# Moving the conditioning vector's products from TensorE's attention loop to GpSimd

## The chip, the cores and the metric

One core of a Trainium2 chip runs one program. Its engines are TensorE (PE in the profile; PEld is its weight load), VectorE (DVE), ScalarE (ACT), GpSimd (POOL) and SyncE (SP). They run at the same time and wait for each other by semaphores only. The metric is the device time of one execution in microseconds (us), lower is better.

## The reference, cut to what matters

Two transformer blocks, batch 1, 512 positions, width 1024, all fp32. The change concerns the modulation of the second block, which is made from the conditioning vector `c` alone:

```python
c_act = jax.nn.silu(c)                                   # 1 x 1024
mod = (c_act @ w_ada[l] + b_ada[l])[:, None, :]          # w_ada: 1024 x 6144
shift1, scale1, gate1, shift2, scale2, gate2 = jnp.split(mod, 6, axis=-1)
h = rmsnorm(x, norm1_w[l]) * (1.0 + scale1) + shift1
...
x = x + gate1 * mix
h = rmsnorm(x, norm2_w[l]) * (1.0 + scale2) + shift2
x = x + gate2 * peer(h, ...)
```

`mod` doesn't depend on the first block. It is needed for the first time when the second block begins.

## The kernel before, in words

The kernel works through stages, one after the other: projection ("win"), retention and compression ("cmp"), compressed attention, the attention loop, the output products ("wout"), the up and down products of the first feed-forward, and then the second block: its input products ("win2"), its states, output products ("wout2"), queries and expert products. Barriers end some of the stages (`PHASE_ENDS`).

Dense products run in a precision of three products: each fp32 weight chunk of 128 x 1024 is loaded by SyncE into the ring `RAW` (`load`, line 633; four slots), split by ScalarE into a high part `WH` (`split_high`, line 246) and by VectorE into a low part `WL` (`split_low`, line 254), and TensorE multiplies high by high, low by high and high by low (`mm3`, line 261). All chunks are numbered in one sequence (`PHASES`, line 45), so that the ring runs on from stage to stage; the splits run some three chunks ahead of the products (`LEAD`).

The attention loop (TensorE line 1702, ScalarE 838, VectorE 1197) goes over 64 units: 2 branches x 4 query tiles (t) x 8 heads. In step s TensorE makes the scores of unit s against t+1 key tiles (line 1706) with the mask (1709), then the transposes of unit s-1 (1737), then the product with the values of unit s-2 (1748). VectorE takes the maximum of the scores (1202), ScalarE the exponential (844), and the two take turns in copying the transposed tile out of PSUM (851, 1209). After each eighth unit VectorE scales and adds the result (1236 to 1243).

Between the scores and the transposes of a step this loop also carries the products for `mod`. `w_ada` is 48 chunks: 6 vectors v of 8 chunks k (`ada_at`, line 568: ten steps for each v, eight of them with a chunk). The silu of `c` is spread out over 128 columns and split in two parts (`CAB`, lines 825 and 1156). Each chunk takes six products of 512 columns (line 1720), so that a PSUM bank pair holds the vector, the same in all partitions. For the gates (v = 2, 5) VectorE adds it to `GATE` (line 1220), which GpSimd had filled with the bias. For the other four, ScalarE copies it to `MODROW` (859), TensorE turns it into eight columns by one-column products (1726), and VectorE adds bias and norm weight into `MOD` (1225, 1228).

Later, in the second block, `turn_act(act, "pre3", ...)` (line 899) uses MOD[:, 0:16], "pre4" (964) the rest; line 387 reads `GATE` 0 and line 1559 `GATE` 1. "pre2", "pre3", "pre4" are the transitions between two dense stages: `norm_act`, `norm_dve` (line 378) add the product to the rows of X and normalize them, `turn_pe` (line 403) transposes the four row tiles, and `turn_act`, `turn_dve` scale and split the result.

GpSimd's queue (line 688) issues a few loads, each behind a wait: among them `ROW` with "nf_post" after the first row norm (line 725), the levels (727), and later, for the expert stage, elementwise work (737, 748).

## Time and profile before

| | us |
|---|---|
| median of 3 runs | 2852.19 |
| lowest, highest | 2852.02, 2855.08 |
| the profiled execution | 2854.3 |
| its span, first to last instruction | 2852.4 |
| TensorE busy in it | 2713.1 (95%) |
| VectorE, ScalarE, GpSimd busy in it | 1506.2, 1079.0, 199.8 |

Times of the trace are in us from the start of the span. The page gives busy time by engine, the windows give it for a stretch of time together with the granted TensorE clock (1.00 is 2.4 GHz, 0.50 is 1.2 GHz). In a timeline the brackets tell how long the engine had been idle and what it had waited for. TensorE's matmul times overlap, so the distance of two starts says what one costs.

### The profile page before, as it was taken

How to read it: one execution, taken by the hardware profiler on the slowest of the kernel's cores; microseconds unless marked ns; L12 is line 12 of the kernel's file. 1: busy time of each engine (PE TensorE's matmuls, PEld its weight loads, DVE VectorE, ACT ScalarE, POOL GpSimd, SP SyncE). 2: the span in 40 equal slices, each digit the busy share in tenths (PEclk: the TensorE clock that was granted, in tenths of full speed). 3: DMA queues.
4: the chain of work that ended last, by engine and by line, in shares of the span. 5: the costliest groups of instructions: out<-in, count | busy, mean ns of one | idle time of the engine just before them, and what ended most of it. 6: DMA issues, size and time to landing. Idle time of an engine off the chain costs nothing.

```text
span 2852.4 us, 33034 instructions
## 1 busy us (share of the span) xinstructions
PE 2713.1 (95%) x12865; PEld 2252.8 (79%) x12865; DVE 1506.2 (53%) x2472; ACT 1079.0 (38%) x1464; POOL 199.8 (7%) x127
## 2 busy tenths in 40 slices
PE   7977998899998998799999999999999999999997
PEld 6866776788787886678888888888888888888886
DVE  4363554555534565467767756565424444444444
ACT  4342443433324443343333345555423333333332
POOL 0020000000000000000001233333100000000000
PEclk9986999999999999899999999999999999999999
DMA  5321342232322221233435535454656565556552
GB/s 174 96 85 52 119 133 76 80 96 96 96 89 81 89 74 45 70 119 104 130 126 152 152 124 218 160 221 162 230 204 222 184 197 202 187 187 205 196 185 81
DMA packets 142363, 392.09 MB, mean 137 GB/s; under 512 B 10944, under 2 KB 44752, under 8 KB 140688
## 3 DMA queue, kind: packets, MB, share of 16 engines
q1 hardware_dynamic: 88032, 274.86, 29.4%
q10 hardware_dynamic: 51904, 102.77, 10.4%
q0 software_dynamic: 2288, 12.54, 1.2%
q8 instruction: 96, 1.57, 0.2%
q14 instruction: 43, 0.35, 0.0%
HBM read 318.82 MB, written 71.30 MB: 137 GB/s over the span
## 4 chain that ended last, share of the span: by engine, by line
PE 92%; DVE 4%; ACT 2%; DMA 1%; issue 1%; DVEq 0%; POOL 0%; ACTq 0%; SPq 0%; POOLq 0%
PE PS L263 27%; PE PS L264 26%; PE PS L265 26%; PE PS L1868 4%; PE PS L1706 2%; PE PS L1748 1%; PE PS L1785 1%; PE PS L1737 1%; PE PS L1709 1%; PE PS L410 1%; PE PS L1846 1%; PE PS L1684 0%; DMA RAW<-in_w_in 0%; DVE X L399 0%; DMA A<-in_subk 0%
## 5 line engine op out<-in xcount | busy, mean ns | idle before, releaser
L258 DVE TENSOR_TENSOR WL<-RAW,WH 128x1024 fp32r<-128x1024 f32 x462 | 593.4, 1286 | 807.6 <-ACT WH L252 761.3
L263 PE MATMUL PS<-HH,WH 128*128 128x512 f32 x1696 | 669.2, 395 | 16.9 <-DMA A<-in_subk 6.7
L252 ACT ACTIVATE WH<-RAW 128x1024 fp32r<-128x1024 f32 x462 | 486.3, 1053 | 469.1 <-PE PS L265 448.2
L264 PE MATMUL PS<-HL,WH 128*128 128x512 f32 x1696 | 661.9, 390 | 0.0
L265 PE MATMUL PS<-HH,WL 128*128 128x512 f32 x1696 | 661.6, 390 | 0.0
L263 PE MATMUL PS<-WH,WGH 128*128 128x512 f32 x1024 | 398.5, 389 | 0.7 <-ACT ROW L987 0.7
L264 PE MATMUL PS<-WL,WGH 128*128 128x512 f32 x1024 | 398.3, 389 | 0.0
L265 PE MATMUL PS<-WH,WGL 128*128 128x512 f32 x1024 | 398.3, 389 | 0.0
L263 PEld LDWEIGHTS PS<-HH,WH 128*128 128x128 f32 x1696 | 319.8, 189 | 84.4 <-DMA A<-in_subk 7.0
L265 PEld LDWEIGHTS PS<-HH,WL 128*128 128x128 f32 x1696 | 319.4, 188 | 66.6
L264 PEld LDWEIGHTS PS<-HL,WH 128*128 128x128 f32 x1696 | 319.8, 189 | 63.6
L263 PEld LDWEIGHTS PS<-WH,WGH 128*128 128x128 f32 x1024 | 192.2, 188 | 40.9 <-ACT ROW L987 1.1
L265 PEld LDWEIGHTS PS<-WH,WGL 128*128 128x128 f32 x1024 | 192.2, 188 | 40.0
L264 PEld LDWEIGHTS PS<-WL,WGH 128*128 128x128 f32 x1024 | 192.2, 188 | 39.9
L1021 ACT ACTIVATE WGH<-A 128x512 fp32r<-128x512 f32 x128 | 80.9, 632 | 238.0 <-DVE A L1538 238.0
L263 PE MATMUL PS<-WH,HH 128*128 128x512 f32 (+1 forms) x352 | 137.1, 390 | 22.0 <-DVEq L205 20.3
L1542 DVE TENSOR_TENSOR WGL<-A,WGH 128x512 fp32r<-128x512 f32 x128 | 88.6, 692 | 94.0 <-ACT WGH L1021 94.0
L264 PE MATMUL PS<-WL,HH 128*128 128x512 f32 (+1 forms) x352 | 135.9, 386 | 0.0
L265 PE MATMUL PS<-WH,HL 128*128 128x512 f32 (+1 forms) x352 | 135.5, 385 | 0.0
L1009 ACT ACTIVATE A<-PS 128x512 f32<-128x512 f32 x128 | 125.9, 1107 | 14.4 <-PE PS L1868 14.4
L987 ACT ACTIVATE ROW<-PS 128x512 f32<-128x512 f32 x64 | 38.3, 598 | 231.7 <-PE PS L265 231.7
L1868 PEld LDWEIGHTS PS<-A 128*128 128x128 f32 x1024 | 121.7, 192 | 3.7
(316 smaller groups left out, 2942.4 us busy)
## 6 DMA issues: line engine op xcount, KB each, us to landing
RAW<-in_peer_u SPq DMA_DIRECT2D x128, 512.0 KB, 3.6
RAW<-in_peer_v SPq DMA_DIRECT2D x128, 512.0 KB, 4.1
gate_matrices<-A ACTq DMA_DIRECT2D x8, 4096.0 KB, 12.5
A<-gate_matrices ACTq DMA_DIRECT2D x32, 1024.0 KB, 7.8
A<-acts ACTq DMA_DIRECT2D x32, 1024.0 KB, 11.4
RAW<-in_w_ada SPq DMA_DIRECT2D x48, 512.0 KB, 4.1
RAW<-in_ffn_up SPq DMA_DIRECT2D x44, 512.0 KB, 3.4
acts<-GATE SPq DMA_DIRECT2D x64, 256.0 KB, 2.9
```

Of the source, the lines that this page charges most:

```text
L252: nc.scalar.activation(WHr[:, slot(c), 0:w], RAW[:, slot(c), 0:w], ACT.Copy).then_inc(sem("high_done"), 1)
L258: nc.vector.tensor_tensor(WLr[:, slot(c), 0:w], RAW[:, slot(c), 0:w], WH[:, slot(c), 0:w], ALU.subtract).then_inc(sem("low_done"), 1)
L263: nc.tensor.matmul(out, L[0], R[0], start=first, stop=False)
L264: nc.tensor.matmul(out, L[0], R[1], start=False, stop=False)
L265: return nc.tensor.matmul(out, L[1], R[0], start=False, stop=last)
L410: last = nc.tensor.transpose(PS[:, k, t * P:(t + 1) * P], src[:, t, k * P:(k + 1) * P], ident)
L987: nc.scalar.activation(ACTED[k % 4], PS[:, 5 + k % 3, :], ACT.Gelu).then_inc(sem("gelu_done"), 1)
L1009: nc.scalar.activation(dst, PS[:, b % 4, :].rearrange("p (t n) -> p t n", t=4), ACT.Copy) .then_inc(sem("gm_stored"), 1)
L1021: nc.scalar.activation(WGHr[:, v % 4, :], WF[:, v % 2, :], ACT.Copy).then_inc(sem("w_high"), 1)
L1542: nc.vector.tensor_tensor(WGLr[:, v % 4, :], WF[:, v % 2, :], WGH[:, v % 4, :], ALU.subtract)\
L1706: nc.tensor.matmul(PS[:, s % 2, 0:(t + 1) * P], QT[0:64, h, t * P:(t + 1) * P], KT[0:64, 2 * b + h // 4, 0:(t + 1) * P], start=True, stop= ...
L1868: last = nc.tensor.matmul(PS[:, b % 4, j * P:(j + 1) * P], OHA[:, r, :], OHB[:, r, :], start=True, stop=True)
```

## The change

The 48 chunks of `w_ada` leave the sequence of chunks, and with them the loads on SyncE's queue, the 48 splits on ScalarE and on VectorE, 288 products on TensorE, CAB, MODROW and the four turns of the attention loop. Instead ScalarE scales the silu of `c` by 128 (`CA`), and GpSimd does this after the attention loop: it fetches `w_ada` in 96 pieces of 128 x 512 into two buffers (`HALVES`), multiplies each by the value of `c` that belongs to its partition, and adds it to a row tile (`ADA` for four vectors, `GATE` for two). At the end each row tile must still be summed over its 128 partitions. TensorE does that with the constant matrix "mean" (all 1/128): for the four vectors ahead of the transposes of "pre3", as 32 one-column products, after which VectorE makes `MOD` in four operations; for the gates as four products of 512 columns after the second chunk of "win2", which ScalarE copies back to `GATE`. The memory of `ADA` and `HALVES` is free during wout, up and down.

```diff
-PHASES = [("win", 24), ("cmp", 8), ("ada", 6 * NK), ("wout", 8), ("up", 2 * NF), ("down", NF),
+PHASES = [("win", 24), ("cmp", 8), ("wout", 8), ("up", 2 * NF), ("down", NF),
...
+        def modulation(dve, link):
+
+            dve.wait_ge(sem("mod_summed"), 1)
+            nc.vector.tensor_tensor(MOD[:, 0:16], PS[:, 0, 0:16], par("bada", 0, 16), ALU.add)
+            link(nc.vector.tensor_tensor(MOD[:, 16:32], PS[:, 0, 16:32], par("bada", 24, 40), ALU.add))
+            nc.vector.scalar_tensor_tensor(MOD[:, 8:16], MOD[:, 8:16], 1.0, par("n1"), ALU.add, ALU.mult)
+            nc.vector.scalar_tensor_tensor(MOD[:, 24:32], MOD[:, 24:32], 1.0, par("n2"), ALU.add, ALU.mult)\
+                .then_inc(sem("mod_taken"), 1)
+
         def norm_dve(dve, link, tag):
...
+                if t == NT and tag == "pre3":
+                    modulation(dve, link)
                 if t >= 1:
                     inverse = inverse_of_rows(dve, link, tag, t - 1)
...
         def turn_pe(pe, tag, src):
+            if tag == "pre3":
+                pe.wait_ge(sem("ada_added"), 6 * 2 * NK)
+                pe.wait_ge(sem("rows_weighted"), NT * ADDED.index(tag) + 1)
+                for n in range(4 * NK):
+                    at = slice((n % NK) * P, (n % NK + 1) * P)
+                    last = nc.tensor.matmul(PS[:, 0, n:n + 1], ADA[n // NK][:, at], con("mean")[:, 0:1], start=True, stop=True)
+                last.then_inc(sem("mod_summed"), 1)
+                pe.wait_ge(sem("mod_taken"), 1)
...
-            c0 = FIRST["ada"]
-            ada = dr["w_ada"].rearrange("(k p) (v n) -> v k p n", p=P, v=6)
-            with sp.Fori(0, 6) as i:
-                for k in range(NK):
-                    load((c0 + k, i, NK), ada[i, k])
...
-            pool.wait_ge(sem("rows_weighted"), NT)
-            pool.dma_start(ROW[:, :], dr["nf_post"].partition_broadcast(P)).then_inc(sem("row_landed"), 16)
+            ada = dr["w_ada"].rearrange("(k p) (v h n) -> k v h p n", p=P, v=6, h=2)
+            pieces = [(k, v, h) for k in range(NK) for v in range(6) for h in range(2)]
+
+            def fetch(n):
+                pool.dma_start(HALVES[:, n % 2, :], ada[pieces[n]]).then_inc(sem(f"ada_landed{n % 2}"), 16)
+
+            after(pool, "attention")
+            pool.wait_ge(sem("ca_ready"), 1)
+            pool.wait_ge(sem("gb_landed"), 32)
+            fetch(0)
+            fetch(1)
+            scaled = 0
+            for n in range(len(pieces)):
+                k, v, h = pieces[n]
+                if n == 48:
+                    pool.wait_ge(sem("rows_weighted"), NT)
+                    pool.dma_start(ROW[:, :], dr["nf_post"].partition_broadcast(P)).then_inc(sem("row_landed"), 16)
+                pool.wait_ge(sem(f"ada_landed{n % 2}"), 16 * (n // 2 + 1))
+                row = GATE[:, v // 3, :] if v % 3 == 2 else ADA[MODDED.index(v)]
+                row = row[:, 512 * h:512 * h + 512]
+                if k == 0 and v % 3 < 2:
+                    ins = nc.gpsimd.tensor_scalar(row, HALVES[:, n % 2, :], CA[:, k:k + 1], None, ALU.mult)
+                else:
+                    nc.gpsimd.tensor_scalar(HALVES[:, n % 2, :], HALVES[:, n % 2, :], CA[:, k:k + 1], None, ALU.mult)\
+                        .then_inc(sem("ada_scaled"), 1)
+                    scaled += 1
+                    pool.wait_ge(sem("ada_scaled"), scaled)
+                    wait(pool, "ada_added", n - 11)
+                    ins = nc.gpsimd.tensor_tensor(row, row, HALVES[:, n % 2, :], ALU.add)
+                ins.then_inc(sem("ada_added"), 1)
+                if n + 2 < len(pieces):
+                    pool.wait_ge(sem("ada_added"), n + 1)
+                    fetch(n + 2)
...
             link(nc.scalar.activation(CA, par("c"), ACT.Silu))
-            nc.scalar.activation(CABr[:, 0], CA.unsqueeze(2).to_broadcast([P, NK, P]), ACT.Copy)\
-                .then_inc(sem("ca_high"), 1)
+            nc.scalar.activation(CA, CA, ACT.Copy, scale=float(P)).then_inc(sem("ca_ready"), 1)
...
-                v, k = ada_at(s)
-                if v < 6 and k < NK:
-                    split_high(act, (FIRST["ada"] + NK * v + k + LEAD, 0, 0))
-                elif v in (0, 1, 3, 4) and k == NK:
...
+            act.wait_ge(sem("mod_taken"), 1)
             turn_act(act, "pre3", lambda k: MOD[:, 8 + k:9 + k], lambda k: MOD[:, k:k + 1])
...
+                if m == 2:
+                    act.wait_ge(sem("gate_summed"), 1)
+                    for g in range(2):
+                        nc.scalar.activation(GATE[:, g, :].rearrange("p (a b) -> p a b", a=2), PS[:, 4 + 2 * g:6 + 2 * g, :],
+                                             ACT.Copy).then_inc(sem("gate_kept"), 1)
...
-            split_low(dve, (FIRST["wout"] + LEAD - 1, 0, 0))
             barrier(dve, "attention")
...
-                    for half in range(2):
-                        hs = slice(half * 512, (half + 1) * 512)
-                        last = mm3(PS[:, 6 + half, :], (CABr[:, 0, k, :], CABr[:, 1, k, :]),
-                                   (WHr[:, slot(c), hs], WLr[:, slot(c), hs]), k == 0, k == NK - 1)
-                    last.then_inc(sem("chunk_used"), 1)
...
+                if m == 1:
+                    for g in range(2):
+                        for h in range(2):
+                            last = nc.tensor.matmul(PS[:, 4 + 2 * g + h, :], con("mean"), GATE[:, g, 512 * h:512 * h + 512],
+                                                    start=True, stop=True)
+                    last.then_inc(sem("gate_summed"), 1)
+                if m == 10:
+                    pe.wait_ge(sem("gate_kept"), 2)
```

## Rows read from the trace of the kernel before

**Rows 1.** The page, section 1: busy us, share of the span, instructions.

```profile
PE 2713.1 (95%) x12865; PEld 2252.8 (79%) x12865; DVE 1506.2 (53%) x2472; ACT 1079.0 (38%) x1464; POOL 199.8 (7%) x127
```

**Rows 2.** Windows: us, busy time by engine (instructions), granted clock, DMA share, GB/s.

```profile
248.20:465.90 217.70, 211.04 (x1024) 157.60 (x1024) 116.91 (x184) 101.70 (x212) 0.00 (x0) 0.90 0.36 114
248.20:264.50 16.30, 16.29 (x43) 11.84 (x43) 4.85 (x8) 5.00 (x13) 0.00 (x0) 0.50 0.20 63
408.00:418.00 10.00, 9.64 (x33) 7.76 (x34) 3.07 (x8) 3.09 (x7) 0.00 (x0) 0.52 0.02 9
418.00:464.00 46.00, 44.43 (x247) 32.29 (x245) 26.00 (x38) 19.73 (x40) 0.00 (x0) 0.99 0.30 92
514.00:538.00 24.00, 14.21 (x69) 12.23 (x68) 20.14 (x33) 18.30 (x35) 0.56 (x1) 0.79 0.20 66
538.00:789.00 251.00, 245.76 (x1067) 202.88 (x1068) 134.85 (x159) 86.61 (x115) 0.00 (x0) 0.98 0.29 93
908.00:912.00 4.00, 0.23 (x1) 0.23 (x2) 3.96 (x8) 2.60 (x6) 0.00 (x0) 0.78 0.00 0
```

**Rows 3.** Timeline of VectorE in the attention loop: start us, us, line, operation.

```profile
343.89 0.69 DVE L1202 TENSOR_REDUCE MISC<-PS 128x1 f32<-128x512 f32 x1 [0.33 <-PE PS L1709]
...
347.92 0.69 DVE L1202 TENSOR_REDUCE MISC<-PS 128x1 f32<-128x512 f32 x1 [2.20 <-PE PS L1709]
...
350.53 0.69 DVE L1202 TENSOR_REDUCE MISC<-PS 128x1 f32<-128x512 f32 x1 [0.19 <-PE PS L1709]
...
376.49 0.29 DVE L1202 TENSOR_REDUCE MISC<-PS 128x1 f32<-128x128 f32 x1 [0.47 <-PE PS L1709]
...
377.47 0.29 DVE L1202 TENSOR_REDUCE MISC<-PS 128x1 f32<-128x128 f32 x1 [0.49 <-PE PS L1709]
...
391.47 0.42 DVE L1202 TENSOR_REDUCE MISC<-PS 128x1 f32<-128x256 f32 x1
...
403.18 0.42 DVE L1202 TENSOR_REDUCE MISC<-PS 128x1 f32<-128x256 f32 x1
...
423.97 0.56 DVE L1202 TENSOR_REDUCE MISC<-PS 128x1 f32<-128x384 f32 x1 [1.79 <-PE PS L1709]
...
427.44 0.56 DVE L1202 TENSOR_REDUCE MISC<-PS 128x1 f32<-128x384 f32 x1
...
458.63 0.69 DVE L1202 TENSOR_REDUCE MISC<-PS 128x1 f32<-128x512 f32 x1 [1.32 <-PE PS L1709]
```

**Rows 4.** Timeline of VectorE at the end of the attention loop.

```profile
462.77 0.20 DVE L1236 RECIPROCAL MISC<-MISC 128x8 f32<-128x8 f32 x1 [1.20 <-PE PS L1748]
...
464.66 1.22 DVE L258 TENSOR_TENSOR WL<-RAW,WH 128x1024 fp32r<-128x1024 f32 x1
```

**Rows 5.** Chain of waits (start us, us, what), and TensorE's timeline at pre3.

```profile
378.25 1.95 PE PS L1726 x16
408.36 3.53 PE PS L1726 x16
...
911.77 0.47 PE L410 MATMUL PS<-CON,A 128*128 128x128 f32 x1 [4.36 <-DVE A L393]
```

**Rows 6.** Timeline of TensorE's weight loads, line 1828, 512-column fp32 products.

```profile
1143.21 0.19 PEld L1828 LDWEIGHTS PS<-A,CON 128*128 128x128 f32 x1 [0.24 <-issue]
```

**Rows 7.** GpSimd's lines (busy us, mean ns, idle before), and DMA issues (KB, us to landing).

```profile
L748 POOL TENSOR_TENSOR X<-CON,A 128x1024 f32<-128x1024 f32 x32 | 68.6, 2143 | 131.5 <-DVE A L1529 117.0 <-ACT X L1032 14.5
...
L707 POOL COPY HH_scratch<-A 128x256 f32<-128x256 f32 x8 | 2.8, 404 | 19.4 <-PE PS L1634 19.4
...
L725 POOL DMA_DIRECT2D ROW<-in_nf_post x1 | 0.6, 561 | 339.5 <-DVE A L393 339.5
...
ROW<-in_nf_post POOLq DMA_DIRECT2D x1, 512.0 KB, 3.9
```

**Rows 8.** VectorE's lines in 790 to 899 us, then in 1650 to 2048 us.

```profile
L258 DVE TENSOR_TENSOR WL<-RAW,WH 128x1024 fp32r<-128x1024 f32 x20 | 24.5, 1226 | 76.1 <-ACT WH L252 76.1
...
L258 DVE TENSOR_TENSOR WL<-RAW,WH 128x1024 fp32r<-128x1024 f32 x54 | 85.7, 1591 | 99.5 <-ACT WH L252 89.7 <-ACT X L1032 9.9
```

46 lines of the change are left out of this document (3 added, 43 removed).

## The prediction, made before the changed kernel ran

> **What bounds the kernel now.** I read the page first: TensorE is busy for 95% of the span, GpSimd for 7% [rows 1]. Every microsecond of products is therefore a microsecond of time, unless something makes TensorE wait. Then I read the windows of the stretch that the change touches, the attention loop, from 248.2 to 465.9 us [rows 2]: 217.7 us in which TensorE is busy for 211.0 us, VectorE for 117 and ScalarE for 102, at a mean granted clock of 0.90. The loop is bound by TensorE too, and part of it runs at the lower clock level. Third, the timeline of VectorE's maximum, which follows the scores of each unit, gives the length of a step with a w_ada chunk in it and without one [rows 3]. GpSimd is an idle engine that can take work at no cost as long as nobody waits for it.
>
> **Part 1, the attention loop without the chunk products.** A step is as long as the distance of two maxima [rows 3]. Three key tiles (here called t=3, 512 keys): 343.89 to 347.92 is 4.03 us with a chunk, 347.92 to 350.53 is 2.61 us without, so a chunk's six products cost 1.42 us. t=2 with a chunk: 3.47 us, less 1.42 is 2.05. t=1: four steps with a chunk from 391.47 to 403.18 are 2.93 each, less 1.42 is 1.51. t=0 without a chunk: 376.49 to 377.47, 0.98 us. Eight units of each t and two branches: 16 x (2.61 + 2.05 + 1.51 + 0.98) = 114.4 us.
>
> Is TensorE still the last to be ready when the products are gone? From one unit's scores to its transposes lie the maximum and the exponential, and a unit's transposes come after the next unit's scores. for t=3 the bare step is 2.61 us as soon as the chunks are gone, and TensorE is busy for 44.4 of 46 us in the stretch that ends with them [rows 2]; for t=0 the 0.98 us already is the bare step. So I take the bare steps as they stand, and add what the chunks now cover:
> - The block that VectorE runs after every eighth unit (lines 1236 to 1243, some 1.9 us, the distance from 462.77 to 464.66 in [rows 4]) delays the next maximum. Behind a long step this is covered, behind t=0 and t=1 steps it is not: I take four stalls of about 1 us, 4 us (0 to 8).
> - The clock. From 248.2 to 264.5 the granted clock is 0.50, the 1.2 GHz level, although TensorE is busy for 16.29 of 16.30 us there [rows 2]; the stage before it leaves TensorE half idle. I keep these 16.3 us at the lower level. A t=0 step at that level would cost some 1.8 us instead of 0.98 (its products twice as long), so nine steps lose 0.8 us each: 8 us (3 to 30, because thinner steps may raise the clock later).
> - Both ends. The last maximum is at 458.63 [rows 3]; a step of 2.61 us after it, at 461.2, the 64 steps are used up. VectorE ends its block at 464.66 and then spends 1.22 us on a split that the change drops there [rows 4]: 3.4 us and no split. For the start, where nothing overlaps yet, I add one and a half t=0 steps, 1.4 us: 4.8 us.
>
> Sum: 114.4 + 4 + 8 + 4.8 = 131.2 us against 217.7. Part 1 is -86.5 us, with ends at -95 and -60. This also contains the four MODROW turns, their waits, and the stretches at the lower clock level that came after them (the last is 408 to 418 at 0.52 [rows 2], with the turn of line 1726 at 408.36 [rows 5]); the diff takes out the thin one-column products ahead of them. ScalarE's and VectorE's 48 splits and SyncE's 48 loads go as well: none is late in the loop, so nothing is added for them. The two operations that built CAB sit before the loop, beside the compressed scores (line 1684) that TensorE makes without them, and give nothing.
>
> **Part 2, GpSimd's 96 pieces.** They start when the attention loop ends and TensorE asks for all 96 when it has finished the down products, at 907.4 us in the times of before (the transposes start at 911.77 after 4.36 us idle [rows 5]). The stretch between the two does not change its length, so 907.4 - 465.9 = 441 us, some 4.6 us for each piece. The price of one: the multiply, one input of 512 columns, lies between the copy of 256 columns twice (0.40 x 2 = 0.8 us) and less; I take 0.7. The add, two inputs, is half of a 128x1024 one of 2.14 us mean [rows 7]: 1.07. Issuing the next fetch is 0.56 us [rows 7]. Three waits on its own semaphores, for which no row of GpSimd stands, between nothing and 0.2 us each: 0.3. That is 2.6 us; collisions with VectorE (part 4) add perhaps 0.5: 3.1. A fetch lands 3.9 us after its issue (512 KB [rows 7]; these are 256 KB), and two are in flight: two pieces take the larger of twice 3.1 and of 3.9 + 2.6 = 6.5 us, so 3.25 each and 312 us in all. GpSimd ends about 125 us before it is asked. Cost on the path: zero, cover 125 us. If that cover is gone (over 4.6 us for each piece), each further 0.1 us costs 9.6 us. The moved ROW load (nf_post) waits behind piece 48, about 160 us after the loop, while its reader comes after 435 us: nothing. The level load stands behind all pieces, as late as before. By the Trainium skill, GPSIMD Engine Reference, section Performance versus the Vector engine, elementwise work belongs on VectorE and a two-input fp32 add of 2048 columns takes 4.5 us on GpSimd; 2.14 us for 1024 columns here agrees with it. By that page the add of a piece would be an estimated 1.1 us, and the sum the same: the rule against this placement matters only where somebody waits for GpSimd.
>
> **Part 3, what TensorE gets back.** Before the transposes of "pre3" it now makes 32 one-column fp32 products, 64 passes. The 16 passes of line 1726 took 1.95 us once and 3.53 us in the stretch with a clock of 0.52 [rows 2, 5], so 64 take 7.8 or 14.1 us. TensorE has only the idle 4.36 us before 911.77 to hide them. In before the clock falls in that gap (0.78 in the mean of 908 to 912 [rows 2]), at about 910; I take 19 passes at 0.122 us and 45 at 0.22: 12.2 us, end at 919.6. Then VectorE makes four operations of 8 or 16 columns with two links, about 1 us, and only then TensorE turns: 920.7 instead of 911.8. The last row norm, which the same wait holds up on VectorE, needs 1 us more and the fourth tile only. ScalarE's new wait stands in front of transposes that it awaits anyway. +9 us (4 if the clock stays up, 11 if it is low throughout).
>
> The gate sums are four 512-column fp32 products, 8 passes of 0.43 us (weight loads of 0.19 us with 0.24 us between them [rows 6]): 3.4 us in the middle of a stage in which TensorE never waits, so +3.4 us (3.4 to 7). ScalarE's two copies behind m=2 (some 1 us each) fall into its idle time. The wait before m=10 is met long before.
>
> **Part 4, VectorE beside a busy GpSimd.** VectorE's 128x1024 split takes 1.23 us while GpSimd is idle and 1.59 us in the mean of 1650 to 2048 us, where GpSimd works a third of the time [rows 8]. In the up and down loops VectorE has slack (busy for 135 of the up loop's 251 us [rows 2]), so a longer split costs nothing there. It does around the norm before the up products ("pre2"), where VectorE is the busier engine, 20.1 of 24 us [rows 2]: four X additions (line 399) and four normalizations (line 375), each with GpSimd busy perhaps 60% of the time. Eight times some 0.3 us: +2.5 us (0 if they never meet, 8 if each waits for a whole add of part 2). The Trainium skill, SBUF — State Buffer, in its section on port contention, says that GpSimd and a VectorE instruction with two SBUF inputs, or in a two-port mode, exclude each other for a whole instruction. The longer splits agree. By that rule, if each of the eight met a full add, it would be 8.6 us.
>
> **The sum.** -86.5 + 9 + 3.4 + 2.5 = -71.6 us. The profiled execution took 2854.3 us at a span of 2852.4; the median of the runs is 2852.2, and both move alike: 2852.2 - 71.6 = 2780.6, and I say 2781 us.
>
> **The rivals.**
> - A, the lower clock lasts. With only small products the t=0 and t=1 units of both branches might run at 1.2 GHz. They would lose 0.8 us in 16 steps and 1.4 in 16 steps, 35 us, of which 8 are counted: 2808 us. For it speaks that 16.3 us of full work did not raise the clock at the start; against it, that the bare t=3 steps stayed at the upper level (0.99 in [rows 2]), and that the falls came with one-column products.
> - B, GpSimd becomes the bound (the other side). If a piece takes over 4.6 us, TensorE waits at "pre3" for all 96. At 5.35 us for each piece, 0.75 us x 96 = 72 us are lost and the gain is gone; at 5.6 us it is slower than before, 2877 us. It needs both operations to collide with VectorE each time (VectorE's split of 1.2 us in front of each would give 2.6 + 2.4 = 5.0 us) and a slow landing on top. The 2.14 us mean of the add, collisions included, speaks against it.
> - C, VectorE held up by GpSimd is late for the products, not only in "pre2": the up loop's six exposed operations in four chunks would have to wait 1.5 us each to fill its 21.8 us. 3 us more in each start of a loop: 2790 us.
> - D, the stalls that the chunks covered are longer (exponential and maximum last in every step of t=0 and t=1, 0.3 us in 32 steps): 2791 us.
>
> **Chances.** Forecast 0.62 (2766 to 2795 us), A 0.14, B 0.06 (half of it beyond the old time), C 0.06, D 0.12. The range that holds 8 in 10, with the unknown prices on both sides: 2765 to 2810. A change of 0.2%, 5.7 us, is about what a measurement of this kernel can tell from none. Faster by more: 0.96; within: 0.01; slower: 0.03.
>
> **What would show it.** The windows of the attention loop: 131 us instead of 217.7, bare steps of 2.61 and near 1 us, a single low-clock stretch at its start. The lines of GpSimd: two groups of about 0.7 and 1.1 us, the last one over 100 us before TensorE's sums. The timeline at "pre3": 64 thin passes, the clock falling in them, the transposes 9 us later against the end of the down products. The lines of VectorE: a longer split between the loop's end and GpSimd's end only. I would be wrong if TensorE waits for GpSimd's adds, if the clock row shows 0.5 beyond the first 20 us of the loop, or if TensorE's idle time in the up loop grows.

## The result, and the profile after

The kernel after takes 2866.3 us (median of 6 runs, 2863.8 to 2869.9), the kernel before 2854.0 beside it (2852.0 to 2855.7). The ratio is 1.0045, 95% interval [1.0034, 1.0057]: slower by 0.45%, where 2781 was forecast. The profiled execution took 2866.0 us at a span of 2864.2. Of all executions below one, of 3480 us at a mean granted clock of 0.73, was slow throughout, and no comparison uses it.

The windows of the kernel after, the same stretches as [rows 2] at their new places (columns as there). First the attention loop, then the clock just ahead of it and a piece of its middle, then the stretch around the norm "pre2", the up loop, and the transition "pre3":

```profile
246.90:457.40 210.50, 209.44 (x672) 146.52 (x672) 59.06 (x127) 50.07 (x160) 0.00 (x0) 0.51 0.00 0
240.00:247.00 7.00, 4.30 (x16) 3.27 (x14) 2.49 (x4) 0.00 (x0) 0.00 (x0) 0.84 0.00 1
290.00:346.00 56.00, 56.00 (x172) 37.06 (x171) 13.80 (x23) 11.74 (x31) 0.00 (x0) 0.50 0.00 0
510.00:535.00 25.00, 12.24 (x62) 10.28 (x61) 23.43 (x32) 17.69 (x32) 22.45 (x19) 0.81 0.33 101
535.00:786.00 251.00, 245.31 (x1067) 202.43 (x1067) 140.66 (x159) 85.84 (x115) 225.78 (x176) 0.98 0.51 155
904.00:932.00 28.00, 23.22 (x119) 19.24 (x119) 14.66 (x25) 18.02 (x29) 0.59 (x1) 0.82 0.12 38
```

The first row is the result. Of 1024 products 672 are left, VectorE's and ScalarE's work in the loop has halved, and yet the loop is only 6 us shorter (211.8 us from its first scores to the first product behind it, 217.8 before), because the granted clock is 0.51 where it was 0.90: 1.2 GHz nearly from end to end. TensorE is busy for 209.4 of the 210.5 us of the window. The loop did get lighter; the clock took back what that gave.

The timeline of VectorE's maximum (line 1234 now) gives the steps. Two of one key tile, then two of four:

```profile
250.15 0.29 DVE L1234 TENSOR_REDUCE MISC<-PS 128x1 f32<-128x128 f32 x1 [1.48 <-PE PS L1719]
251.83 0.29 DVE L1234 TENSOR_REDUCE MISC<-PS 128x1 f32<-128x128 f32 x1 [1.15 <-PE PS L1719]
...
430.60 0.69 DVE L1234 TENSOR_REDUCE MISC<-PS 128x1 f32<-128x512 f32 x1 [3.31 <-PE PS L1719]
435.48 0.69 DVE L1234 TENSOR_REDUCE MISC<-PS 128x1 f32<-128x512 f32 x1 [4.19 <-PE PS L1719]
```

1.68 us where the bare step of [rows 3] is 0.98, and 4.88 where it is 2.61. The steps of two and three key tiles (distances 2.75 and 3.81, at 381.24 and 401.34 in the same timeline) stand against 1.51 and 2.05. Sixteen of each are 210 us.

From there on I followed the same points in both timelines (the last column is the sum so far, after less before):

| point | before | after | difference |
|---|---|---|---|
| first scores of the loop | 248.21 | 246.93 | -1.3 |
| first transpose behind the loop ("mix") | 465.99 | 458.71 | -7.3 |
| first up product | 537.97 | 534.19 | -3.8 |
| end of the down products | 907.3 | 903.1 | -4.2 |
| first transpose of "pre3" | 911.77 | 913.08 | +1.3 |
| GpSimd's last row | 2847.56 | 2851.89 | +4.3 |
| end of the span | 2852.4 | 2864.2 | +11.8 |

The up loop's products are not disturbed: TensorE is busy for 245.3 of 251 us, against 245.8 in [rows 2], with GpSimd busy for 226. The largest term after the clock is in the last two lines of the table, and no step of the prediction has it: 7.5 us between GpSimd's last row and the end of the span. The last instructions of the program, all recorded at line 142, show where they are. GpSimd's closing DRAIN (an instruction of its sequencer, so it counts as busy time nowhere and stands in no timeline) takes 1.54 us before and 8.97 after (ns, least, median and most; then the start in us):

```profile
L142 POOLq DRAIN  x1: 1539/1539/1539, 2850.7 to 2850.7; - x1
...
L142 POOLq DRAIN  x1: 8973/8973/8973, 2855.0 to 2855.0; - x1
```

GpSimd's lines (busy us, mean ns, idle before):

```profile
L755 POOL TENSOR_SCALAR A<-A,MISC 128x512 f32<-128x512 f32 x88 | 158.0, 1795 | 4.3 <-DMA A<-in_w_ada 0.3
L760 POOL TENSOR_TENSOR A<-A 128x512 f32<-128x512 f32 x56 | 83.4, 1489 | 4.7
...
L736 POOL DMA_DIRECT2D A<-in_w_ada x96 | 56.5, 589 | 300.4 <-DVEq L205 272.5 <-POOL A L760 16.6 <-POOL GATE L760 8.9
L760 POOL TENSOR_TENSOR GATE<-GATE,A 128x512 f32<-128x512 f32 x32 | 45.4, 1420 | 2.7
```

And its timeline at the end of the pieces, and at the end of the kernel:

```profile
856.22 1.63 POOL L760 TENSOR_TENSOR GATE<-GATE,A 128x512 f32<-128x512 f32 x1
907.85 0.59 POOL L766 DMA_DIRECT2D ROW<-in_levels  x1 [50.00 <-DVE A L402]
...
2851.89 0.53 POOL L797 DMA_DIRECT2D out<-X  x1 [1.35 <-DVE X L1580]
```

The pieces run from 458.96 to 857.85, 4.15 us each, and TensorE asks for them at 903.09: 45 us of cover are left, not 125, and nobody waits. TensorE's timeline there:

```profile
902.86 0.39 PE L265 MATMUL PS<-WH,GSL 128*128 128x512 f32 x1
903.09 9.36 PE L420 MATMUL PS<-CON,A 128*128 128x1 f32 x64
913.08 3.25 PE L429 MATMUL PS<-CON,A 128*128 128x128 f32 x14 [0.63 <-DVE MISC L384]
```

64 passes in 9.36 us, the four VectorE operations, and the transposes 10.0 us after the down products, where it was 4.5.

### The profile page after: what moved, and what is told of

Same layout as the page of the kernel before. It is cut to its first block, busy times and chain, and to the rows that moved or that the text cites. A ratio compares the mean times of both kernels' runs of the same rounds, so it can differ in the third digit from the quotient of the medians.

```text
span 2864.2 us, 32473 instructions
## 1 busy us (share of the span) xinstructions
PE 2721.4 (95%) x12585; PEld 2250.9 (79%) x12585; DVE 1470.7 (51%) x2419; ACT 1028.4 (36%) x1414; POOL 555.7 (19%) x407
## 4 chain that ended last, share of the span: by engine, by line
PE 92%; DVE 4%; ACT 2%; DMA 1%; issue 0%; DVEq 0%; POOL 0%; SPq 0%; ACTq 0%; POOLq 0%
PE PS L263 26%; PE PS L264 25%; PE PS L265 25%; PE PS L1868 4%; PE PS L1716 3%; PE PS L1740 2%; PE PS L1729 1%; PE PS L1777 1%; PE PS L1719 1%; PE PS L1846 0%; PE PS L1695 0%; DMA RAW<-in_w_in 0%; PE PS L429 0%; DVE X L410 0%; DMA A<-in_subk 0%
## 5 line engine op out<-in xcount | busy, mean ns | idle before, releaser
L258 DVE TENSOR_TENSOR WL<-RAW,WH 128x1024 fp32r<-128x1024 f32 (+1 forms) x414 | 541.0, 1309 | 798.6 <-ACT WH L252 752.3
L252 ACT ACTIVATE WH<-RAW 128x1024 fp32r<-128x1024 f32 (+1 forms) x414 | 436.1, 1054 | 469.4 <-PE PS L265 448.8
L755 POOL TENSOR_SCALAR A<-A,MISC 128x512 f32<-128x512 f32 x88 | 158.0, 1795 | 4.3 <-DMA A<-in_w_ada 0.3
```

Source lines behind the costliest of these rows:

```text
L252: nc.scalar.activation(WHr[:, slot(c), 0:w], RAW[:, slot(c), 0:w], ACT.Copy).then_inc(sem("high_done"), 1)
L258: nc.vector.tensor_tensor(WLr[:, slot(c), 0:w], RAW[:, slot(c), 0:w], WH[:, slot(c), 0:w], ALU.subtract).then_inc(sem("low_done"), 1)
L755: nc.gpsimd.tensor_scalar(HALVES[:, n % 2, :], HALVES[:, n % 2, :], CA[:, k:k + 1], None, ALU.mult)\
```

## The experiments

Two theories came out of the trace. T1: the loop ran at the lower level for want of the dense products that the change took away; they had paid for themselves by the clock. T2: the last 7.5 us are GpSimd's, from the transfers that its queue issued. All experiments but two start from the kernel after. An execution is one timed run of the kernel; only one of each experiment's was profiled. "Ballast" is a product whose result is thrown away. Its operand is the high part of a w_out chunk, which lies ready, and its output a PSUM bank that nobody reads:

```diff
+        def fill(pe, n):
+            w = WHr[:, slot((FIRST["wout"] + 2, 0, 0)), :]
+            for i in range(n):
+                nc.tensor.matmul(PS[:, 6 + i % 2, :], w[:, 0:128], w[:, 0:512], start=True, stop=True)
```

Where a run's executions differ among themselves by whole steps of 40 us and more, they are listed one by one: the clock in the loop came out differently from one execution to the next, and a median of such a run says little.

**Ballast ahead of the loop alone.**

```diff
+            pe.wait_ge(sem("low_done"), number((FIRST["wout"] + 2, 0, 0), 1))
+            fill(pe, 12)
             barrier(pe, "compressed attention")
```

> The kernel after, with twelve products of 128x512 added on TensorE ahead of the barrier that closes the compressed attention (operand: a weight chunk whose high half lies ready; output: a PSUM bank that nobody reads). They fill the idle 2.7 us in which TensorE waits for VectorE ahead of the loop, where the clock stands at its upper level; the results are thrown away. Theory T1 (the loop's own small products cannot hold the upper level from its first steps on, whatever comes before): the clock is at 0.5 again within a few us, loop 205 to 212 us, time 2862 to 2867. Rival T1b (the clock falls at the loop's start because TensorE stood idle for 2.7 us just before, and the steps alone would hold it): the loop's clock stays near 1.0, loop 110 to 130 us, time near 2780.

2865.3 us, 1.0055 times the kernel before, 95% interval [1.0038, 1.0072] (written so from here on). The clock was at 1.00 up to 250.7 us and at 0.50 from there to the loop's end. The 2.7 us of idle time ahead of the loop are not needed to bring it down: with them filled it is lost in the bare first steps, after a pause of TensorE of 0.34 us that ends at 246.71.

**Ballast in each of the 64 steps too.**

```diff
                 if s < len(units):
                     b, t, h = units[s]
+                    fill(pe, 1)
                     wait(pe, "at_exp", s - 1)
```

> As the run before, and one product of 128x512 more in each of the 64 steps of the attention loop, ahead of the step's scores. T1 (the loop ran at the lower level for want of dense products): the clock is at its upper level for at least the longer steps; the loop takes 131 us plus 64 x 0.22 us = 145 us where all of it is, and the time comes to about 2800; with the shortest steps still at the lower level about 2825. Rival (one product a step is too little, or the level hangs on something other than TensorE's own work): clock 0.5 throughout, loop 212 + 64 x 0.43 = 239 us, time about 2894.

2792.4 us (four executions, 2789.2 to 2794.6), 0.9791 [0.9775, 0.9808]. 64 more products in the loop and twelve ahead of it made the kernel 74 us faster. The loop's window:

```profile
248.99:385.90 136.91, 133.95 (x736) 89.69 (x735) 58.29 (x128) 50.05 (x160) 0.00 (x0) 1.00 0.00 1
```

T1 holds so far: at the upper level the loop takes 137 us with 14 us of ballast in it (64 x 0.22). Bare, that is 123 us. This version beats both kernels; the last experiment shows how far that can be relied on.

**GpSimd's pieces left out.**

```diff
-            fetch(0)
-            fetch(1)
-            for n in range(len(pieces)):
...
+            for n in range(4):
+                nc.gpsimd.memset(ADA[n], 0.0).then_inc(sem("ada_added"), 1)
```

> The kernel after with the conditioning vector's products left out: GpSimd loads, multiplies and adds nothing, the four weighted-sum rows are zeros, the gates keep only their bias. All else stays: no products in the loop, the sums over partitions, the wait and the gate sums. If the clock in the loop has nothing to do with GpSimd (T1), the loop is again 211 us at 0.5. T2 (the last 7.4 us come from GpSimd's closing drain, which grows with the transfers that its queue issued): the span ends within 2 us of the last row of GpSimd's work plus its landing as in the kernel before, and the time is 2866.3 - 7.4 - 2 to 4 us of contention gone = 2855 to 2858. Rival (GpSimd's work beside the dense stages costs VectorE and TensorE more than the traces suggest): below 2853. Rival to T2 (the end has another cause): 2862 to 2865.

2854.3 us, 1.0009 [0.9999, 1.0018] (the rows are zeros, so its result is wrong). Its window of the loop:

```profile
246.00:458.00 212.00, 209.82 (x671) 146.79 (x671) 60.55 (x128) 50.08 (x160) 0.00 (x0) 0.50 0.00 0
```

And the last row of GpSimd's timeline:

```profile
2850.53 0.53 POOL L777 DMA_DIRECT2D out<-X  x1 [1.28 <-DVE X L1560]
```

The loop is at 0.50 with GpSimd's pieces gone: the fall is not GpSimd's doing. The span is 2855.4, so it ends 4.9 us after the last GpSimd row, as in the kernel before (2847.56 to 2852.4, 4.8); the kernel after needs 12.3. Without the 96 loads those 7.4 us are gone, and the closing DRAIN takes 1.54 us again. What GpSimd costs beside the dense stages is small: from the loop's end to the first up product it is 73.65 us here and 75.48 after (72.0 before), and 1.1 us in the up and down stages. The 1.7 us that this stretch is longer than before even here are not GpSimd's; 1.2 of them lie between the first transpose behind the loop and the first "wout" product (12.0 us, 10.7 before).

**The same 96 loads, but small.**

```diff
-                pool.dma_start(HALVES[:, n % 2, :], ada[pieces[n]])
+                pool.dma_start(HALVES[:, n % 2, 0:16], ada[pieces[n]][:, 0:16])
...
+            nc.gpsimd.memset(A[:, 21504:22528], 0.0).then_inc(sem("halves_clear"), 1)
```

> The kernel after with each of GpSimd's 96 loads cut from 512 columns to 16 (8 KB in place of 256 KB); the rest of the two buffers is zero, so the conditioning vector's products are wrong for 496 columns of 512. Count and order of the loads, and all the arithmetic, stay. If the closing drain grows with the number of transfers or of their packets, the end stays as in the kernel after (11 to 12 us between the last GpSimd row and the end of the span); if with the bytes, it falls to about 4.6 us as in the kernel before, and the span is 7 us shorter. VectorE's and TensorE's times beside GpSimd are expected within 1 us of the kernel after: the loads share no queue with the weights.

A single execution, 2864.0 us. The last GpSimd row is at 2849.89, the span 2862.2: 12.3 us, as with the full loads, and the DRAIN is 8.97 us to the nanosecond. Not the bytes, then.

**Half the loads,** on the kernel with ballast in every step.

```diff
             def fetch(n):
-                pool.dma_start(HALVES[:, n % 2, :], ada[pieces[n]])...
+                if n % 4 < 2:
+                    pool.dma_start(HALVES[:, n % 2, :], ada[pieces[n]])...
...
-                pool.wait_ge(sem(f"ada_landed{n % 2}"), 16 * (n // 2 + 1))
+                pool.wait_ge(sem(f"ada_landed{n % 2}"), 16 * (n // 4 + 1))
```

> The kernel of the 2792.4 us run (twelve products ahead of the loop, one dense product in each step) with every second pair of GpSimd's loads left out, 48 transfers in place of 96; the pieces without a load of their own take the rests of the piece before, so the conditioning vector's products are wrong. T2 (the closing drain costs 7.4 / 96 = 0.077 us for each transfer that GpSimd's queue issued): the end of the span is 3.7 us nearer to the last GpSimd row, time 2788 to 2789. If the drain is one fixed price once the queue has held more than some number: 2792. Loads and arithmetic beside the dense stages are otherwise as before; up to 1 us less contention.

2788.0 us (2785.5 to 2791.9), 0.9779. GpSimd's last row is at

```profile
2774.86 0.53 POOL L804 DMA_DIRECT2D out<-X  x1 [1.28 <-DVE X L1587]
```

and the span 2783.6: 8.7 us. The closing DRAIN:

```profile
L142 POOLq DRAIN  x1: 5462/5462/5462, 2777.9 to 2777.9; - x1
```

GpSimd's queue issued 18, 66 and 114 transfers in the kernel before, here and in the kernel after. The end took 4.8, 8.7 and 12.3 us, the DRAIN in it 1.54, 5.46 and 8.97: 0.08 us for each transfer, whatever its size. In all traces of this document the DRAIN has one of these three lengths, by the number of transfers alone. T2 is shown for that number (each load of a piece goes to all 128 partitions, so transfers and their parts are not told apart).

**Where does the ballast have to be?** The reading of [rows 2] that bare steps of four key tiles hold the upper level (0.99 from 418 to 464, of which the last six steps have no chunk) suggested that the shorter steps alone would need it. First in the steps of one and two key tiles, without and with the twelve ahead of the loop:

```diff
                     b, t, h = units[s]
+                    if t < 2:
+                        fill(pe, 1)
```

> The kernel after with one thrown-away product of 128x512 in each step of the loop whose tile is one of the first two (32 of 64 steps; the steps of one and two blocks), and none ahead of the loop. Two readings of the run with the ballast in all 64 steps (loop 134.6 us, time 2792.4 us). H (the steps of three and four blocks hold the upper level by themselves once it is reached): the level is reached some us into the loop; those 32 steps take 2.05 and 2.61 us, 0.3 us less than with ballast: time 2792.4 - 32 x 0.29 = 2783, plus up to 4 us at the start: 2783 to 2787. N (no bare step holds it): about half the loop at the lower level, the 32 longer steps 3.8 and 4.9 us in place of 2.35 and 2.90: 2792.4 + 16 x 1.45 + 16 x 2.0 = 2848.

> As the run with ballast in the 32 shorter steps, and twelve thrown-away products ahead of the loop as well. H: the clock is at its upper level from the loop's first step; time 2781 to 2785, 0 to 4 us under the run without the twelve. N (bare steps of three and four blocks do not hold it): 2848, as there.

Then in the first eight steps alone (the condition is `s < 8`), and in all sixteen of one key tile (`t == 0`), both with the twelve:

> The kernel after with twelve thrown-away products ahead of the loop and one more in each of its first 8 steps alone (all eight of one block). H1 (steps of two and more blocks hold the upper level once it is reached, steps of one block do not): the clock is at its upper level to the end of the first branch (about 65 us of loop), falls in the bare steps of one block that open the second branch, and does not come back: the second branch takes 105 us in place of 60, time about 2785 + 45 = 2830. H0 (any bare step holds it once reached): the whole loop is at the upper level, time about 2781 to 2785, which is the time that the forecast gave. N (no bare step holds it): the clock falls within a few us of step 8, time 2856 to 2864.

> The kernel after with twelve thrown-away products ahead of the loop and one more in each of the 16 steps of one block, in both branches. H1 (steps of two and more blocks hold the upper level): the whole loop is at the upper level, 16 x 0.22 = 3.5 us of ballast in it, time about 2783. If the steps of two blocks do not hold it: the clock falls in steps 8 to 15 and the rest of each branch runs at the lower level: about 2855. If the clock falls there and steps of three or four blocks raise it again: between the two.

```
ballast                             executions, us                              level in the profiled loop
none (kernel after)                 2864 2864 2866 2867 2868 2870                0.5 from 249.0
t < 2, none ahead                   2881 2882 2885, and one of 3480                  0.5 from 247.0
t < 2, twelve ahead                 2827 2830 2835 2836                          1.0 to 315.4, then 0.5
s < 8, twelve ahead                 2820 2822 2823, and seven of 2861 to 2865    1.0 to 312.7, then 0.5
t = 0, twelve ahead                 2780 2823 2868 2868                          1.0 to the end (the 2780)
```

The times stand on a ladder with rungs 40 to 46 us apart: both branches at the upper level, one, or none. In the second row the level is never raised: ballast in the short steps at 1.2 GHz does not lift it. Where it is raised, bare steps of two to four key tiles hold it for tens of us, but not surely. I had named clear cases (held, not held, held in part), and the same kernel gives one or another of them from one execution to the next. The one execution in which it held to the end has the forecast's loop with 16 products of ballast in it, and its time is the forecast's:

```profile
247.42:372.57 125.15, 120.85 (x688) 84.60 (x687) 58.14 (x128) 50.04 (x160) 0.00 (x0) 1.00 0.00 1
```

**Half the ballast** in each step: the moving operand is `w[:, 0:256]` in place of `w[:, 0:512]`, twelve full ones ahead.

> The kernel after with twelve thrown-away products of 128x512 ahead of the loop and one of 128x256 in each of its 64 steps, so half the ballast of the run that gave 2792.4 us. If half the dense work is enough to hold the upper level, the loop takes 134.6 - 64 x 0.11 = 127.6 us and the time is 2785 in every execution. If it is on the edge, as the runs without ballast in the longer steps were, executions fall on a ladder: 2785, about 2785 + 42 to 45 where the clock falls for one branch, and 2872 where it falls for both.

Executions of 2832, 2836, 2836, 2888, 2890 and 2891 us: the edge case, on the two slower rungs only. Half the ballast in all steps is no better than the full one in some. In the profiled execution (2888 us) the level fell at 250.3, in the third step. TensorE's longest pause since the ballast ahead of the loop is this one, of 0.17 us:

```profile
249.06 0.33 PE L1745 MATMUL PS<-CON,A 128*128 128x128 f32 x1 [0.17 <-ACT A L894]
```

**Ballast in each step, none ahead** (the kernel of 2792.4 us without `fill(pe, 12)`).

> The kernel after with one thrown-away product of 128x512 in each of the 64 steps, and none ahead of the loop: the run of 2792.4 us without its twelve. U (once the clock has fallen in the 2.7 us of idle time and the first steps, one dense product a step does not raise it; it only holds it): clock 0.5 throughout, loop 212 + 64 x 0.43 = 239 us, time 2866 + 27 = 2893, in line with the 2881 to 2885 of the run with ballast in 32 steps. R (one a step raises it too, a little later): 2793 to 2805. Were it to rise only in the longer steps: between.

2899.2 us (2897.8 to 2900.3), 1.0166 [1.0149, 1.0183], clock 0.50 from 246.8 to the loop's end. The same 64 products that are worth 74 us when the clock is up at the loop's start cost 33 when it is not. With the run of 2792.4 us this settles T1: the loop is the same, the clock is not, and the times are 107 us apart. Either level can last through the whole loop, and in these two runs what TensorE did before it decided which.

**Small products as ballast,** four of 128x64 in fp32 in each step, with and without the twelve dense ones ahead.

```diff
+                nc.tensor.matmul(PS[:, 6 + i % 2, 0:64], w[:, 0:128], w[:, 0:64], start=True, stop=True)   # w in fp32, four times
```

> The kernel after with twelve thrown-away products of 128x512 ahead of the loop and, in each step, four small fp32 products of 128x64 (the form of the loop's own last products) in place of the one dense product: TensorE is kept busy as long or longer, with work of the same kind as its own. W (what holds the clock is the kind of product, not the time that TensorE is busy): the clock falls to 0.5 within a few us of the loop's start, as without ballast; the four take about 0.9 us a step at that level: loop 212 + 58 = 270, time about 2920, at least 2890. B (any busy time holds it): clock 1.0, 64 x 0.45 = 29 us of ballast at the upper level, time about 2778 + 29 = 2807.

> The kernel after with four small fp32 products of 128x64 in each step and none ahead of the loop: the run of 2829.1 us without its twelve dense ones. That run held the upper level from the start. If small products can hold a level but not raise it, the clock falls in the idle gap and the first steps and stays at 0.5: four cost about 0.9 us a step there, 2866 + 58 = 2924, at least 2900. If TensorE being busy is all that counts, it rises within the first steps: 2829 to 2835.

2829.1 us (2826.5 to 2832.0) with the twelve, 2977.4 without. The window of the run with them:

```profile
244.00:415.00 171.00, 170.81 (x1168) 137.80 (x1166) 56.69 (x125) 49.47 (x159) 0.00 (x0) 1.00 0.00 1
```

And of the run without:

```profile
250.00:550.00 300.00, 300.00 (x1113) 240.76 (x1113) 55.76 (x120) 47.96 (x155) 0.00 (x0) 0.50 0.00 1
```

TensorE is busy all but 0.2 us in both, and one is at 1.00, the other at 0.50 for 300 us. So my reading that only dense products hold the level (W) falls: small ones hold it, at nearly four times the price (by the times 0.8 us a step, where a dense one costs 0.22, and not the 0.45 I had put), but they do not raise it. At the lower level they cost 1.7 us a step, twice what I had put. The run of 2829 us is also the only one at the upper level whose timeline has no pause of TensorE over 0.1 us in the loop, but for one of 0.29 us that ends at 415.19, in its last step.

**A dense burst at step 8,** 24 products, nothing else (`if s == 8: fill(pe, 24)`).

> The kernel after with 24 thrown-away products of 128x512 in one burst at step 8 of the loop (the first step of two blocks), where the clock is at its lower level, and none elsewhere. D (a stretch of dense products raises the level, and steps of two to four blocks then mostly hold it): the clock goes to 1.0 within the burst's 10 us; the rest of the first branch takes about 50 us in place of 92; the bare steps that open the second branch then let it fall or not: 2866 + 8 - 42 = 2832 where it falls, 2787 where it does not. U (nothing raises it in the loop but products in every step, as in the kernel before): 2866 + 24 x 0.43 = 2876.

2871.1 us (2867.5 to 2872.2). It does raise the level, and some four steps later it is lost, so neither forecast holds. TensorE's timeline; the level is 1.0 from 263.1 to 273.4 us:

```profile
259.58 7.38 PE L271 MATMUL PS<-WH 128*128 128x512 f32 x24
...
272.57 0.44 PE L1737 MATMUL PS<-CON,A 128*128 128x128 f32 x2 [0.61 <-ACT A L888]
...
274.47 0.47 PE L1727 MATMUL PS<-MASK 128*128 128x128 f32 x1
```

The middle row has the first pause since the burst: TensorE waited 0.61 us for ScalarE's exponential. In the last one a mask product takes 0.47 us again, where it takes 0.33 at the upper level.

**Does every fall stand behind such a pause?** I listed the pauses of TensorE in the loops of all profiled executions beside the times at which the level fell. The kernel before has four of over 0.5 us inside its loop, all at the one-column products of line 1726, which wait for ScalarE's copy:

```profile
277.37 2.36 PE L1726 MATMUL PS<-CON,A 128*128 128x1 f32 x16 [0.84 <-ACT A L859]
...
311.03 1.95 PE L1726 MATMUL PS<-CON,A 128*128 128x1 f32 x16 [1.00 <-ACT A L859]
```

The level fell at 278.7, 312.9, 381.1 and 408.4, each time within 3 us of one (the others are in [rows 5]). Two experiments from the kernel before are on this: twelve products ahead of its loop, and, with them, one in each step that has no chunk (into the scores' own bank, before the scores are made).

```diff
                     wait(pe, "at_exp", s - 1)
+                    if s % 10 >= 8 or s >= 60:
+                        nc.tensor.matmul(PS[:, s % 2, :], CABr[:, 0, 0, :], CABr[:, 0, 0:4, :]...)
```

> The kernel before with twelve thrown-away products of 128x512 added on TensorE ahead of the barrier that closes the compressed attention; its own products stay in the loop. If the first 16 us of its loop are at the lower level only because TensorE stood idle for 2.7 us ahead of them, the clock is at its upper level from the loop's start and the time falls by about 8 us, to 2844 to 2847. If the long waits behind the products of the first steps bring it down anyway, 2851 to 2855. In both cases it stays over 50 us behind the kernel after with one dense product a step.

> The kernel before with twelve thrown-away products ahead of the loop and one of 128x512 in each of the 16 steps of its loop that carry no product of the conditioning vector. If the falls inside its loop come from those bare steps, the whole loop is at the upper level: a mean clock of 0.90 means that about a fifth of 218 us was at the lower level, some 44 us in which 22 us are lost; with 3.5 us of ballast the time is 2852.9 - 22 + 3.5 = 2834, in every execution, and the kernel after with ballast in every step (2792.4) stays 42 us ahead: that would be what moving the products is worth once the clock is held in both. If the falls have another cause (the waits behind the longer steps), 2851 to 2856, as with the idle gap filled alone.

2851.8 us, 0.9993 [0.9982, 1.0004], and 2851.1 us, 1.0000 [0.9989, 1.0012]. Both start at the upper level and both lose it at all four turns. In the timeline of the second the first turn is

```profile
269.18 3.31 PE L1737 MATMUL PS<-CON,A 128*128 128x1 f32 x16 [0.56 <-ACT A L865]
```

and the window behind it, in which the level is down with the chunks' dense products in it, before they bring it back:

```profile
269.50:283.20 13.70, 13.70 (x46) 10.79 (x46) 5.46 (x10) 2.65 (x8) 0.00 (x0) 0.50 0.16 49
```

So the bare steps of the kernel before are not what costs it the clock, and my first reading (2834 us) was wrong. All twelve falls behind the first steps of the three loops stand at the turns. A turn has a pause and thin one-column products, and no run takes one of the two away, so which of them matters was not separated.

**Ballast on both sides of the change of branch** (`if t in (0, 3)`, twelve ahead).

> The kernel after with twelve thrown-away products ahead of the loop and one of 128x512 in each step of one block and of four blocks (32 of 64 steps), so that the change from the first branch to the second has ballast on both sides and the steps of two and three blocks have none. If the falls seen so far come from the turn between the branches alone, the whole loop is at the upper level in every execution, at 2792.4 - 32 x 0.29 = 2783. If the steps of two blocks can lose it too, executions fall on the ladder 2783, about 2826, about 2870.

2829, 2833, 2874 and 2875 us, never the 2783; in the profiled one (2833 us) the level fell at 317.8, behind a pause of 0.54 us that ends at 316.20, in the second branch's first steps, which have ballast. An earlier pause of 0.60 us, at 263.44, had done nothing.

**The sums left out,** on the kernel with ballast in every step.

```diff
-                for n in range(4 * NK):
+                for n in range(0, 4 * NK, 16):
...
-                    for g in range(2):
-                        for h in range(2):
+                    for g in range(1):
+                        for h in range(1):
```

> The kernel of the 2792.4 us run with the sums over partitions nearly left out: 2 of the 64 one-column passes behind the down products, and one of the four gate sums; the modulation is wrong for it. Waits, VectorE's four operations and ScalarE's copies stay. By the trace of the kernel after, the passes with what stands behind them put the turn back by 5.6 us and the gate sums take 3.6: time 2792.4 - 5 - 2.7 = 2785. By the forecast's own sum (9 and 3.4) it is 2792.4 - 9 - 2.6 = 2781.

Executions of 2788, 2834, 2838 and 2839 us. The one on the lowest rung is 4.7 us below the 2792.4 of the kernel that it came from. That is less than the 7.7 I expected and far below the forecast's 11.6, but from a single execution. The other three matter more: the loop is the same as in the run of 2792.4 us, instruction for instruction, and by their times three of four executions lost one branch. In the profiled one (2839 us) it is the second. Its timeline in the first steps of the second branch:

```profile
319.09 0.33 PE L1739 MATMUL PS<-CON,A 128*128 128x128 f32 x1 [0.54 <-ACT A L888]
```

And that of the run with all its sums, in the profiled execution that held:

```profile
320.54 0.33 PE L1739 MATMUL PS<-CON,A 128*128 128x128 f32 x1 [0.54 <-ACT A L888]
```

The same pause of 0.54 us at the same step; after the first the level fell at 320.7, after the second it stayed. One dense product a step therefore held the level in 4 of 4, 4 of 4 and 1 of 4 executions of the three kernels that have this loop (the run of 2792.4 us, the one with half the loads, and this one). The three ran on three different chips, so a difference of the chips may have a part in it; that it is not all of it shows in the table above, where executions of one kernel on one chip differ. Where it holds, the kernel is 60 us faster than before; where it is lost for one branch, 49 of these are gone again (2837 against 2788 here). It is no guarantee.

## Why the prediction was wrong

**The step that failed** is in part 1: "So I take the bare steps as they stand", with the bullet on the clock, which kept 16.3 us at the lower level and let the rest run at the upper one. Two rows bore on it. [Rows 2] show TensorE busy for 16.29 of 16.30 us at 0.50, that is, being busy did not raise the level; I left this to rival A at 0.14. And they show 0.99 up to the loop's end, in which six bare steps of four key tiles stand; but these came behind dense products which had raised it. The row shows that such steps can hold a level. Nothing in the trace showed that they could reach it, and the loop after is at 0.50 from 2 us behind its start. Even with twelve dense products ahead of the loop, which kept the level up at its start, it fell at 250.7. The clock was priced as a tax on the first steps. It is a state, 0.50 for 210 of 212 us, and the run of 2899 against 2792 us shows that it depends on the dense products before.

**The sizes of part 1 were right.** The loop that held the level took 125.2 us with 16 products of ballast (3.5 us), so 121.7 bare; the forecast's 131.2 without its 8 us at the lower level are 123.2. The four stalls, put at 4 us, are four pauses of TensorE of 0.30 to 0.61 us in that loop, 2.1 us in sum. That execution took 2780.4 us. This is the forecast's number, and by luck: the 8 us at the lower level that the forecast counts are not in it, and the 7.4 us at the end that it misses are.

**Rival A** was the right mechanism with a price too low and a chance too low. It put 32 short steps of the two branches at the lower level and got 2808. All 64 were. Its own loss of 0.8 us on a step of 0.98, a factor of 1.82, put on all 114.4 us of bare steps, gives 208 us, with the ends 213, and a time of 2862. The reason against it, "that the falls came with one-column products", was a correct observation (every fall inside the loop of the kernel before is behind one of those turns) with a wrong conclusion, for the change also removed what brought the level back afterwards.

**The end of the kernel** has no step at all in the prediction: +7.4 us, at 0.08 us for each of 96 transfers. I priced the issue of each load on GpSimd's queue, and not the closing DRAIN, whose length goes by the number of transfers.

**Part 2.** The multiply was mis-sized: 1.8 us where I took 0.7 from a copy of 256 columns, twice. The add takes 1.42 to 1.49 us (1.07), the issue 0.59 (0.56), the waits 0.3 (0.3). Sum 4.15 us a piece against 3.25, GpSimd's end 45 us ahead of its reader and not 125 (by the prediction's own 441 and 312 us it should have read 129). The verdict "cost on the path: zero" stood, on a cover a third of what I wrote. Rival B was nearer than its 0.06 suggests: the limit of 4.6 us was missed by 0.45.

**Part 3.** The passes took 9.36 us (12.2), the turn came 5.5 us later against the down products (9). The gate sums measured 3.6 us (3.4). **Part 4.** With GpSimd's work left out the stretch up to the first up product is 1.8 us shorter, 2.9 with the up and down stages; I had 2.5. The collisions that I argued from [rows 8] are there. VectorE's additions and normalizations from 500 to 536 us in the kernel after:

```profile
L410 DVE TENSOR_TENSOR X<-X,A 128x1024 f32<-128x1024 f32 x4 | 6.4, 1608 | 0.0
L375 DVE TENSOR_SCALAR A<-X,MISC 128x1024 f32<-128x1024 f32 x4 | 5.3, 1317 | 0.0
```

Without GpSimd's pieces the means are 1221 and 748 ns. That is 0.4 us more for each addition and 0.6 for each normalization, 3.8 us in all where I had some 2.4; 1.8 of them show in the time of the stretch. Rival C did not come about: TensorE's busy time in the up loop is that of before within 0.5 us. Nor did D: its 9.6 us of further stalls have no room in a loop of 121.7 us.

The sum, redone in the profiled spans: start and loop -7.3, wout and "pre2" +3.5, up and down -0.4, "pre3" +5.5, gate sums 3.6 with -0.6 over the 1900 us that follow, end +7.5: +11.8.

**What stays open.** Every fall of the level that the profiled executions show inside a loop comes in its first steps, behind the 2.7 us of idle time, or within 4 us of a pause of TensorE of 0.17 to 1.12 us; and the run with small ballast behind dense, which has no pause over 0.1 us up to its last step, kept the level in all four executions. In the loops built from the kernel after, five pauses of 0.54 us and more were followed by a fall and seven were not, some of these in the same step of the same loop, while the shortest one with a fall behind it is the 0.17 us of the run with half the ballast. So a pause goes before each fall, its length does not sort the cases, and it is not enough by itself. That it is the cause is argued, not shown: the run without pauses also has more work in it. Why small products hold a level and do not raise it was not found. The Trainium skill says on the page TensorE: Matmul & The Clock Gate, in the section on what is actually happening, that "the default state is throttled, and activity releases the throttle". Of the dense burst the trace agrees (0.50 before it, 1.00 from 263.1). Of the loop itself it does not, if activity is TensorE's busy time as the profile has it: 56.00 of 56.00 us at 0.50 in the kernel after.

## What to carry to other kernels

Before taking dense products out of a loop that TensorE bounds, look at where its clock comes from: if small steps are all that is left, price the loop at both levels, and give the lower one the larger chance unless a row shows the level being raised by such steps alone. If it does fall, one thrown-away dense product in each step, with a burst of them ahead of the loop, can be worth many times its price, but it has to be timed over several executions, since the same code may land on either level. And when work moves to GpSimd with its loads, count the transfers rather than the bytes: each was paid for at the end of this kernel with 0.08 us.

## What the runs showed of the hardware that I had not expected

- The same loop can run from end to end at either clock level. One product of 128x512 in each step gave 2792 us when the level was up at the start and 2899 when it was not.
- TensorE busy for 300 of 300 us with small fp32 products as ballast stayed at 1.2 GHz (0.50); the same loop behind twelve dense products stayed at 2.4 GHz for 171 us.
- A burst of 24 dense products from 259.58 on brought the level up at 263.1; at 273.4 it was gone again.
- One GpSimd multiply of 128x512 by a value for each partition takes 1.57 us in the mean of one group and 1.80 in that of another, longer than the two-input add of the same size (1.42 and 1.49).
- GpSimd's closing DRAIN took 1.54, 5.46 and 8.97 us with 18, 66 and 114 transfers issued by its queue, and the 96 added ones cost the same at 256 KB as at 8 KB.
